# Two blocks of a transformer on one core: a GELU cut in two, constant products on TensorE ahead of turns and late loads, and the first Fourier product one unit later

## The chip, the core and the metric

One core of a Trainium2 chip runs the whole program in one launch. The metric is the time of one execution on the device in microseconds (us). TensorE (PE) multiplies, VectorE (DVE) and ScalarE (ACT) work elementwise, GpSimd (POOL) runs the scan and small parts, and SyncE (SP) issues nearly all DMAs.

## The reference, cut to what matters

Everything is float32, batch 1, 256 tokens, width 2048. `first_block` is a block with modulation, a state space mixer, attention and a gated feed forward part; `second_block` holds an attention layer over latents and context, and a Fourier layer:

```
h = modulate(rms(x, norm1_w), shift1, scale1);  u, q, k, v = split(h @ w_in)
y_ssm = glu(gelu(s5_scan(u) + d * u));  y_att = dilated_attention(q, k, v)
x = x + gate1 * (concat(y_ssm, y_att) @ w_out)
h2 = modulate(rms(x, norm2_w), shift2, scale2)
x = x + gate2 * ((silu(h2 @ w_gate) * (h2 @ w_up)) @ w_down)
... second block, layer 0: attention; layer 1:
a, b = split(h @ w_in_fourier);  o = (silu(b) * real(fft2(a))) @ w_out_fourier
x = layer_norm(alpha * x + gate * o) * g + bias
```

`gelu` is the tanh form. The modulation vectors (shift, scale, gate) are `silu(c) @ w_ada + b_ada`, with weights of 2048 x 12288. All shapes: 256 x 2048 activations, `w_in` 2048 x 4096, feed forward width 5632, Fourier width 4096 in 16 groups of 256.

## The kernel before, in words

**Units.** Each large weight is streamed from HBM in units of two 128-row tiles by 512 columns (512 KB). SP loads a unit into `raw` (a ring of 8, `load`, L186), ACT rounds it to `whi` (`high`, L192, a ring of 4), DVE subtracts to get `wlo` (`low`, L198), and PE multiplies three times: hi by hi, hi by lo, lo by hi (`multiply` L205, 12 products of 512 columns; `multiply_turned` L218, 24 products of 256 columns). `high` waits until the unit four before it has been multiplied. The order in which ACT, DVE, PE and SP take units and all other steps is written out by hand, one list per engine, and every engine works its list strictly in that order.

**Start.** The modulation weights come in 512 KB slots, and `rounds_pe` (L277) multiplies two slots per round into bank 6 (`L297`). After round 31, ACT copies the row out (`set_row_act`), PE turns it into columns (`set_turn_pe`, bank 7), and DVE adds the bias. Then `turn_pe` (L477) transposes the normed x, two tiles a round; DVE scales the result into `h32` (L500), ACT rounds it to `hh` (L507) and POOL subtracts to get `hl` (L512). Round n of the turn must be through POOL before unit n is multiplied. The same turn opens the feed forward part and the Fourier part (in `hidden_pe`, L1955: four rounds ahead of unit 0, then one behind each of the first units).

**In projection** (`in_pe`, `in_act`, `in_dve`, L1231 to L1501). 64 units of `w_in`, with the steps of the eight attention heads and of the state space mixer between them: scores (`a1_scores_pe`), maximum (`a1_max_dve`), `a1_exp_act`, `a1_prob_dve`, and so on. The GELU of half b of the mixer is `y_act` (L895): eight activations of 32 x 256 in two calls, each call four pieces for two values of j (L901). `y_act(act, 0, 2)` stands behind `high` of unit 48, ahead of `high` of unit 49. On DVE, `low` of unit 63 stands behind `a1_max_dve` of head 4. Behind unit 63, PE waits for the last evacuation (`s_inev` 8) and runs rounds 32 to 35 of the next modulation set, whose accumulator is bank 6. The slots of rounds 36 and up are loaded again as rounds 32 and up release them; in SP's list they stand behind the load of the last `w_glu` unit, which waits for `low` of unit 63.

**Feed forward and Fourier** (`Hidden`, `hidden_*`, L1590 to L2001). Chunk c: units 0 to 7 gate columns into banks 0 and 1, 8 to 15 the others into banks 2 and 3, 16 to 23 the down projection of the chunk before. In the Fourier part DVE copies banks 2 and 3 to `ub` (`hidden_up_dve`, L1740), PE multiplies 16 products with the cosine table (`hidden_dft1_pe`, L1899, `L1907`), ACT stores them (`hidden_store_act`, L1682), PE multiplies 32 more (`hidden_dft2_pe`, L1912), and DVE forms the product with the gate (`hidden_product_dve`, L1756). For chunk 0 the copy to `ub` is the last DVE step of chunk 0, the first product stands behind unit 0 of chunk 1, the store behind `high` of unit 2, the second product behind unit 3.

Of the kernel before, what the change touches and what calls it, by code (L numbers as in the profile page):

```python
# [48 lines left out]
U_IN = 0  # L49
# [49 lines left out]
def program(nc, dram, out):  # L99
# [34 lines left out]
    ones = sb(ctx, "ones", [P, P])  # L134
    cols = sb(ctx, "cols", [P, NCOLS])
# [408 lines left out]
    xn = xacc  # L544
# [349 lines left out]

    def y_act(act, b, j0):  # L895

        act.wait_ge(s_yv, b + 1)
        for j in (j0, j0 + 1):
            for pp in range(4):
                o = yT[32 * pp:32 * pp + 32, 4 * b:4 * b + 4].rearrange("p (t f) (m j) -> p t f m j", t=2, j=4)[:, :, :, :, j]  # L900
                ins = nc.scalar.activation(o, u4(b)[32 * j:32 * j + 32, :, pp::4], ACT.Gelu_apprx_tanh)  # L901
        ins.then_inc(s_yg, 1)

    def y_high(act, q):
        if q == 0:
            act.wait_ge(s_mm, U_GLU)
        act.wait_ge(s_yg, 2 * (q // 2) + 2)
        nc.scalar.copy(hh[:, 2 * q:2 * q + 2], yT[:, 2 * q:2 * q + 2]).then_inc(s_yh, 1)
# [298 lines left out]
    def in_sp(sp):  # L1207
# [21 lines left out]
        slots_sp(sp, 96, 104)  # L1229

    def in_pe(pe):  # L1231
        turn_pe(pe, 0, xn, 0, 0, 2)
        for n in range(43):
            if n < 8:
                pe.wait_ge(s_hl, n + 1)
            in_mult(pe, n)
            if n < 6:
                turn_pe(pe, 0, xn, 0, n + 2, n + 3)
            for b in range(2):
                if n == 12 + 8 * b:  # L1240
                    u_turn_pe(pe, b)
                if n == 16 + 8 * b:
                    ends_pe(pe, b)
            if n == 38:
                y_pe(pe, 0)
            if n == 40:
                a1_turn_pe(pe, 0)
# [29 lines left out]
        pe.wait_ge(s_inev, 8)  # L1277
        rounds_pe(pe, 32, 36)
        a1_pturn_pe(pe, 4)
# [31 lines left out]
    def in_act(act):  # L1311
# [31 lines left out]
        for h in range(2):  # L1343
# [3 lines left out]
            a1_qkT_act(act, h + 1)  # L1347
            high(act, U_IN + u + 3)
            if h == 1:
                in_evac(act, 5)  # L1350
# [4 lines left out]
            if h == 0:  # L1355
                y_act(act, 0, 2)
            if h:
# [61 lines left out]
    def in_dve(dve, ch):  # L1419
# [34 lines left out]
        a1_y_dve(dve, 2)  # L1454
        low(dve, U_IN + 62)
        a1_max_dve(dve, ch, 4)
        low(dve, U_IN + 63)
        a1_prob_dve(dve, ch, 4)
# [238 lines left out]
    def hidden_act(act, H, c):  # L1697
        first = isinstance(c, int) and c == 0
# [3 lines left out]
        for j in range(4 if first else 0, 16 if first else 24):  # L1702
# [22 lines left out]
            if not first or j > 4:  # L1725
                high(act, **H.unit(c, j))
            if H.fourier and c == 1 and j == 2:
                hidden_store_act(act, H, 0)
# [58 lines left out]
    def hidden_dve(dve, H, c, q=None, perq=0, lo=0):  # L1787
# [7 lines left out]
        for j in range(4 if first else 0, n):  # L1795
            if not first:
                for r in range(2):
                    if j == PARTS_AT[H.fourier][r]:
                        hidden_low_dve(dve, H, c, r)
                if second and j == 3 and not H.fourier:  # L1800
                    hidden_up_dve(dve, H, 0)
# [40 lines left out]
            if not H.fourier and not first and c <= 8 and j in (18, 20):  # L1842
                dual_sum(dve, 2 * (c - 1) + (j - 18) // 2)
        if H.fourier and first:
            hidden_up_dve(dve, H, 0)
        if q is not None and H.fourier:
# [103 lines left out]
    def hidden_pe(pe, H, c, q=None, perq=0, lo=0):  # L1950
# [3 lines left out]
        if first:  # L1954
            turn_pe(pe, k, xn, kn, 0, 4)  # L1955
        for j in range(16 if first else 24):
# [14 lines left out]
            if not first:  # L1971
                if H.fourier and c == 1 and j == 0:
                    hidden_dft1_pe(pe, H, 0)
                if H.fourier and j == 3:
                    hidden_dft2_pe(pe, H, c - 1)
                if H.fourier and j == 19:
                    hidden_dft1_pe(pe, H, c)
                if H.fourier and c == FCH - 1 and j == 21:
                    hidden_dft2_pe(pe, H, c)
# [1121 lines left out]
    def _(pe):  # L3101
# [12 lines left out]
        for k in range(4):  # L3114
            window_turn_pe(pe, 8 + 2 * k, 10 + 2 * k)
            rounds_pe(pe, 25 + k, 26 + k)
        rounds_pe(pe, 29, 32)
        set_turn_pe(pe, 0)
# [81 lines left out]
```

## Time and profile before

| | before |
|---|---|
| median of 3 runs | 2507.25 us (2505.16 to 2508.38) |
| the profiled execution | 2505.13 us, span 2503.3 us |
| PE busy | 2397.9 us, 96% of the span |
| DVE busy | 1650.0 us, 66% |
| ACT busy | 1044.6 us, 42% |
| mean granted clock of PE | 0.984 |
| DMA | 589.44 MB, 235 GB/s mean |

The span runs from the first to the last instruction. The granted clock is the share of 2.4 GHz that PE was given: 1.00 or 0.50. Matmuls are pipelined, so the duration of one (0.39 us for 512 columns) is longer than the distance to the next one (0.23 us); a row that merges several gives the length of the whole run.

### The profile page before, as it was taken

How to read it: one execution, taken by the hardware profiler on the slowest of the kernel's cores; microseconds unless marked ns; L12 is line 12 of the kernel's file. 1: busy time of each engine (PE TensorE's matmuls, PEld its weight loads, DVE VectorE, ACT ScalarE, POOL GpSimd, SP SyncE). 2: the span in 40 equal slices, each digit the busy share in tenths (PEclk: the TensorE clock that was granted, in tenths of full speed). 3: DMA queues.
4: the chain of work that ended last, by engine and by line, in shares of the span. 5: the costliest groups of instructions: out<-in, count | busy, mean ns of one | idle time of the engine just before them, and what ended most of it. 6: DMA issues, size and time to landing. Idle time of an engine off the chain costs nothing.

```text
span 2503.3 us, 37893 instructions
## 1 busy us (share of the span) xinstructions
PE 2397.9 (96%) x15430; PEld 2053.1 (82%) x15430; DVE 1650.0 (66%) x1869; ACT 1044.6 (42%) x1386; POOL 220.5 (9%) x200
## 2 busy tenths in 40 slices
PE   5899989989999999999999999999979999999996
PEld 1588766569888999888998888888768999999995
DVE  8655545456888888886678566555665585765557
ACT  2444764224333343333343454444443443334432
POOL 0139700011000000000010100000012000000000
PEclk9999999999999999999999999999999999999998
DMA  9855469968999999998554754334546585766561
GB/s 388 331 159 154 146 252 374 401 229 285 356 355 355 380 350 352 348 351 298 167 185 137 236 159 129 104 104 135 169 134 200 196 283 165 240 229 185 152 189 56
DMA packets 257582, 589.44 MB, mean 235 GB/s; under 512 B 20608, under 2 KB 29824, under 8 KB 256128
## 3 DMA queue, kind: packets, MB, share of 16 engines
q1 hardware_dynamic: 257408, 587.02, 67.8%
q8 instruction: 122, 2.00, 0.3%
q14 instruction: 52, 0.43, 0.0%
HBM read 584.85 MB, written 2.10 MB: 234 GB/s over the span
## 4 chain that ended last, share of the span: by engine, by line
PE 90%; DVE 4%; DMA 3%; ACT 1%; issue 1%; POOL 1%; SPq 0%; DVEq 0%; ACTq 0%
PE psum L213 13%; PE psum L225 13%; PE psum L226 12%; PE psum L227 12%; PE psum L215 12%; PE psum L214 12%; PE psum L297 3%; DMA start_slots<-in_w_ada 2%; PE psum L2555 1%; PE psum L1907 1%; DVE wlo L202 1%; PE psum L755 1%; PE psum L487 1%; PE psum L535 1%; PE psum L1921 1%
## 5 line engine op out<-in xcount | busy, mean ns | idle before, releaser
L202 DVE TENSOR_TENSOR wlo<-raw,whi 128x1024 fp32r<-128x1024 f32 (+2 forms) x728 | 879.6, 1223 | 546.7 <-ACT whi L196 543.3
L196 ACT CAST whi<-raw 128x1024 fp32r<-128x1024 f32 (+2 forms) x728 | 738.1, 1022 | 925.4 <-PE psum L227 484.3
L225 PE MATMUL psum<-hh,whi 128*128 128x256 f32 x2688 | 759.6, 283 | 3.1 <-DVE wlo L202 2.5
L226 PE MATMUL psum<-hh,wlo 128*128 128x256 f32 x2688 | 750.5, 279 | 0.0
L227 PE MATMUL psum<-hl,whi 128*128 128x256 f32 x2688 | 750.3, 279 | 0.0
L225 PEld LDWEIGHTS psum<-hh,whi 128*128 128x128 f32 x2688 | 506.8, 189 | 19.9 <-DVE wlo L202 11.7
L227 PEld LDWEIGHTS psum<-hl,whi 128*128 128x128 f32 x2688 | 510.8, 190 | 0.0
L226 PEld LDWEIGHTS psum<-hh,wlo 128*128 128x128 f32 x2688 | 507.0, 189 | 1.9 <-issue 1.0
L213 PE MATMUL psum<-whi,hh 128*128 128x512 f32 (+1 forms) x720 | 292.6, 406 | 11.3 <-DVE wlo L202 7.7
L215 PE MATMUL psum<-whi,hl 128*128 128x512 f32 (+1 forms) x720 | 282.1, 392 | 0.0
L214 PE MATMUL psum<-wlo,hh 128*128 128x512 f32 (+1 forms) x720 | 280.7, 390 | 0.0
L213 PE MATMUL psum<-whi,hidh 128*128 128x512 f32 x544 | 216.5, 398 | 0.0
L215 PE MATMUL psum<-whi,hidl 128*128 128x512 f32 x544 | 212.0, 390 | 0.0
L214 PE MATMUL psum<-wlo,hidh 128*128 128x512 f32 x544 | 211.9, 390 | 0.0
L378 DVE SCALAR_TENSOR_TENSOR powers<-araw,cond,powers 128x1024 f32<-128x1024 f32 x150 | 192.3, 1282 | 8.4
L213 PEld LDWEIGHTS psum<-whi,hh 128*128 128x128 f32 x720 | 136.5, 190 | 62.5 <-issue 22.6
L215 PEld LDWEIGHTS psum<-whi,hl 128*128 128x128 f32 x720 | 136.5, 190 | 29.5
L214 PEld LDWEIGHTS psum<-wlo,hh 128*128 128x128 f32 x720 | 136.9, 190 | 28.5 <-issue 1.9
L475 POOL TENSOR_TENSOR rstd<-ms,mhalf 128x2 f32<-128x2 f32 x5 | 6.4, 1288 | 1553.7 <-DVE ms L2087 633.7
L213 PEld LDWEIGHTS psum<-whi,hidh 128*128 128x128 f32 x544 | 102.1, 188 | 30.8 <-issue 11.0
L215 PEld LDWEIGHTS psum<-whi,hidl 128*128 128x128 f32 x544 | 102.1, 188 | 21.8
L214 PEld LDWEIGHTS psum<-wlo,hidh 128*128 128x128 f32 x544 | 102.2, 188 | 20.7 <-issue 1.0
(394 smaller groups left out, 2400.2 us busy)
## 6 DMA issues: line engine op xcount, KB each, us to landing
araw<-in_ada_w SPq DMA_DIRECT2D x128, 512.0 KB, 6.4
raw<-in_w_in_fourier SPq DMA_DIRECT2D x128, 512.0 KB, 4.1
raw<-in_w_ffn_gate SPq DMA_DIRECT2D x88, 512.0 KB, 8.8
raw<-in_w_ffn_up SPq DMA_DIRECT2D x88, 512.0 KB, 7.5
raw<-in_w_ffn_down SPq DMA_DIRECT2D x88, 512.0 KB, 9.8
raw<-in_w_in_attn SPq DMA_DIRECT2D x88, 512.0 KB, 4.3
araw<-in_w_ada SPq DMA_DIRECT2D x80, 512.0 KB, 7.1
start_slots<-in_w_ada SPq DMA_DIRECT2D x64, 512.0 KB, 8.2
```

Source lines behind the costliest of these rows:

```text
L196: nc.scalar.copy(whi[:, u % SPLITS, 0:kn, 0:w], raw[:, u % RING, 0:kn, 0:w]).then_inc(s_hi, 1)
L202: nc.vector.tensor_tensor(wlo[:, u % SPLITS, 0:kn, 0:w], raw[:, u % RING, 0:kn, 0:w], whi[:, u % SPLITS, 0:kn, 0:w].bitcast(F32), ALU.subt ...
L213: nc.tensor.matmul(o, ah[:, kt + k, a], h, start=(kt + k == first_kt), stop=False)
L214: nc.tensor.matmul(o, ah[:, kt + k, a], lw, start=False, stop=False)
L215: ins = nc.tensor.matmul(o, al[:, kt + k, a], h, start=False, stop=(kt + k == last_kt))
L225: nc.tensor.matmul(o, h, hh[:, kt + k], start=(kt + k == 0 and f % 2 == 0), stop=False)
L226: nc.tensor.matmul(o, lw, hh[:, kt + k], start=False, stop=False)
L227: ins = nc.tensor.matmul(o, h, hl[:, kt + k], start=False, stop=(kt + k == KT - 1 and f % 2 == 1))
L297: ins = nc.tensor.matmul(psum[32 * g:32 * g + 32, SET_BANKS[st][0]], condz[:, vectors - 1, kt, 3 - pi:35 - pi], slot(2 * r + e)[0][:, half ...
L378: ins = nc.vector.scalar_tensor_tensor(out=acc, in0=w, scalar=s, in1=acc, op0=ALU.mult, op1=ALU.add)
L487: ins = nc.tensor.transpose(psum[:, banks[r % 2], j * S + t * P:j * S + t * P + P], xn[:, t, kt * P:(kt + 1) * P], ident[:])
L535: nc.tensor.matmul(psum[:, bank], ones[:], diag[:, r % 2], start=True, stop=True).then_inc(s_grow, 1)
```

## The change

`warm_pe(pe, n, bank)` multiplies `ones` (128 x 128) by the first 256 of the column constants n times into a bank that nothing reads at that time. It is called on PE at these places: two products ahead of each of the rounds 29, 30 and 31 and three behind; five behind the first two rounds of the first turn; two, four and three around rounds 32 to 35; 16 ahead of the feed forward turn and 33 ahead of the Fourier turn, and two and five between their rounds 1 and 2. The GELU call for j = 2, 3 of half 0 becomes two calls of four activations. DVE takes `low` of unit 63 ahead of the maximum of head 4. In the Fourier part the copy to `ub` of chunk 0 moves into chunk 1 ahead of `low` of unit 2, the first product behind unit 1, the store behind `high` of unit 4, the second product behind unit 4.

```diff
-    def y_act(act, b, j0):
+    def y_act(act, b, j0, n=2):
...
-        for j in (j0, j0 + 1):
+        for j in range(j0, j0 + n):
...
-        act.wait_ge(s_yg, 2 * (q // 2) + 2)
+        act.wait_ge(s_yg, 2 * (q // 2) + 3)
...
+    def warm_pe(pe, n, bank):
+
+        for _ in range(n):
+            nc.tensor.matmul(psum[:, bank, 0:256], ones[:], cols[:, 0:256], start=True, stop=True)
+
     def in_pe(pe):
         turn_pe(pe, 0, xn, 0, 0, 2)
+        warm_pe(pe, 5, 6)
...
         pe.wait_ge(s_inev, 8)
-        rounds_pe(pe, 32, 36)
+        rounds_pe(pe, 32, 33)
+        warm_pe(pe, 2, 7)
+        rounds_pe(pe, 33, 34)
+        warm_pe(pe, 4, 7)
+        rounds_pe(pe, 34, 36)
+        warm_pe(pe, 3, 7)
         a1_pturn_pe(pe, 4)
...
             high(act, U_IN + u + 3)
+            if h == 0:
+                y_act(act, 0, 2, 1)
             if h == 1:
                 in_evac(act, 5)
             a1_pT_act(act, h)
...
             if h == 0:
-                y_act(act, 0, 2)
+                y_act(act, 0, 3, 1)
...
         low(dve, U_IN + 62)
+        low(dve, U_IN + 63)
         a1_max_dve(dve, ch, 4)
-        low(dve, U_IN + 63)
...
-            if H.fourier and c == 1 and j == 2:
+            if H.fourier and c == 1 and j == 4:
                 hidden_store_act(act, H, 0)
...
-                if second and j == 3 and not H.fourier:
+                if second and j == (2 if H.fourier else 3):
                     hidden_up_dve(dve, H, 0)
...
-        if H.fourier and first:
-            hidden_up_dve(dve, H, 0)
...
         if first:
-            turn_pe(pe, k, xn, kn, 0, 4)
+            warm_pe(pe, 33 if H.fourier else 16, 6)
+            turn_pe(pe, k, xn, kn, 0, 2)
+            warm_pe(pe, 5 if H.fourier else 2, 6)
+            turn_pe(pe, k, xn, kn, 2, 4)
...
-                if H.fourier and c == 1 and j == 0:
+                if H.fourier and c == 1 and j == 1:
                     hidden_dft1_pe(pe, H, 0)
-                if H.fourier and j == 3:
+                if H.fourier and j == (4 if c == 1 else 3):
                     hidden_dft2_pe(pe, H, c - 1)
...
-        rounds_pe(pe, 29, 32)
+        pe.wait_ge(s_ones, 1)
+        for r in range(29, 32):
+            warm_pe(pe, 2, 7)
+            rounds_pe(pe, r, r + 1)
+        warm_pe(pe, 3, 7)
         set_turn_pe(pe, 0)
```

## Rows read from the trace of the kernel before

**Rows 1.** The page: engine, busy us (share of the span), instructions.
```profile
PE 2397.9 (96%) x15430; PEld 2053.1 (82%) x15430; DVE 1650.0 (66%) x1869; ACT 1044.6 (42%) x1386; POOL 220.5 (9%) x200
```

**Rows 2.** Waits of PE, 0 to 345: us in total, times, longest.
```profile
PE psum L213 <- DVE wlo L202: 7.7, 4, 2.9
```

**Rows 3.** Waits of PE from 1862 to the end.
```profile
PE psum L225 <- DVE wlo L202: 2.5, 1, 2.5
```

**Rows 4.** Timeline of ACT, 240 to 304: start us, us, instruction, [idle before <- releaser].
```profile
269.57 0.59 ACT L1029 COPY xacc<-psum 128x512 f32<-128x512 f32 x1 [3.19 <-PE psum L1021]
...
273.24 1.28 ACT L901 ACT_TABLE_LOAD   x1
274.53 5.34 ACT L901 ACTIVATE bt_x<-proj 32x256 f32<-32x256 f32 x8
279.90 1.04 ACT L196 CAST whi<-raw 128x1024 fp32r<-128x1024 f32 x1
...
282.25 0.91 ACT L1001 ACTIVATE xacc<-xacc,neg 128x256 f32<-128x256 f32 x2
```

**Rows 5.** Timeline of PE, same stretch: units 49 and 50.
```profile
282.37 0.50 PE L213 MATMUL psum<-whi,hh 128*128 128x512 f32 x1 [2.61 <-DVE wlo L202]
...
287.17 0.50 PE L213 MATMUL psum<-whi,hh 128*128 128x512 f32 x1 [1.77 <-DVE wlo L202]
```

**Rows 6.** Timeline of all engines around unit 63, 332 to 366.
```profile
341.73 0.75 DVE L991 SCALAR_TENSOR_TENSOR xacc<-x,cols,psum 128x512 f32<-128x512 f32 x1 [5.53 <-PE psum L981]
...
343.31 1.22 DVE L202 TENSOR_TENSOR wlo<-raw,whi 128x1024 fp32r<-128x1024 f32 x1
...
344.59 0.50 PE L213 MATMUL psum<-whi,hh 128*128 128x512 f32 x1 [2.90 <-DVE wlo L202]
...
346.50 0.63 PE L214 MATMUL psum<-wlo,hh 128*128 128x512 f32 x1
...
348.87 1.01 ACT L1189 COPY proj<-psum 128x1024 f32<-128x1024 f32 x1 [4.53 <-PE psum L215]
...
350.24 1.93 PE L297 MATMUL psum<-araw,cond_windows 128*32 128x512 f32 x16
...
357.25 1.07 PE L297 MATMUL psum<-araw,cond_windows 128*32 128x512 f32 x8 [1.92 <-DMA araw<-in_w_ada]
```

**Rows 7.** Windows: stretch, busy us and count of each engine, PEclk, DMA share, GB/s.
```profile
104.00:105.00 1.00, 0.00 (x0) 0.00 (x0) 1.00 (x2) 0.58 (x1) 0.34 (x1) 0.50 1.06 391
...
289.00:290.00 1.00, 1.00 (x3) 0.76 (x3) 1.00 (x2) 0.00 (x0) 1.00 (x1) 0.50 0.85 328
...
350.00:351.00 1.00, 1.00 (x11) 0.36 (x13) 0.52 (x2) 0.61 (x2) 0.00 (x0) 1.00 0.00 0
...
480.00:500.00 20.00, 20.00 (x103) 11.85 (x102) 9.76 (x9) 5.24 (x5) 0.00 (x0) 1.00 1.04 402
...
1886.00:1887.00 1.00, 1.00 (x7) 1.00 (x6) 1.00 (x2) 0.07 (x1) 0.85 (x1) 0.50 0.00 0
```

**Rows 8.** Timeline of PE, 2440 to 2445: sixteen products of 256 float32 columns.
```profile
2441.42 3.61 PE L1907 MATMUL psum<-dft,ub 128*128 128x256 f32 x16
2444.68 0.58 PE L213 MATMUL psum<-whi,hidh 128*128 128x512 f32 x1
```

**Rows 9.** Timeline of PE at the three turns, 102, 550 and 1878.
```profile
102.11 1.07 PE L487 MATMUL psum<-ident,xacc 128*128 128x128 f32 x8
106.16 0.80 PE L213 MATMUL psum<-whi,hh 128*128 128x512 f32 x1 [2.98 <-POOL hl L512]
...
550.30 1.97 PE L487 MATMUL psum<-ident,xacc 128*128 128x128 f32 x8 [7.59 <-DVE xacc L467]
...
1878.21 1.97 PE L487 MATMUL psum<-ident,xacc 128*128 128x128 f32 x8 [15.16 <-DVE xacc L2876]
```

**Rows 10.** Timeline of DVE and PE at the start of Fourier chunk 1.
```profile
1932.14 1.22 DVE L1748 COPY ub<-psum 128x1024 f32<-128x1024 f32 x1 [8.52 <-PE psum L227]
...
1934.65 0.35 PE L225 MATMUL psum<-hh,whi 128*128 128x256 f32 x1 [2.54 <-DVE wlo L202]
```

## The prediction

> **What bounds the kernel now.** I read the page first: PE is busy 96% of the span, no other engine over 66% [rows 1]. So what shortens the run is PE's idle time, and the time in which its products run at half speed. Then I read the waits of PE by stretch. In the feed forward part there are none. Up to 345 PE waited 7.7 us for `low` in four waits [rows 2], and behind the start of the Fourier part 2.54 us in one [rows 3, 10]. Beside these it waits at the three turns: 2.98, 7.59 and 15.16 us [rows 9]. Last I read windows of one us for the granted clock. It is 1.00 (2.4 GHz) nearly everywhere and 0.50 (1.2 GHz) in a few stretches, each behind such a wait [rows 7]. At 0.50 two `L214` or `L213` products of 512 columns lie 0.43 us apart and at 1.00 they lie 0.23 us apart, so a product loses 0.20 us.
>
> **GELU in two pieces.** Before, ACT idles 3.19 us ahead of the copy of head 0 at 269.57, then takes the table load (1.28) and all eight activations (5.34) in one go, and `high` of unit 49 comes only at 279.90 [rows 4]. PE has finished unit 48 and its small steps by 279.76 (282.37 - 2.61) and stands 2.61 us; unit 50 then stands another 1.77 us, because the exponentials of head 1 came at 282.25, and DVE forms the probabilities of that head ahead of `low` of unit 50 [rows 4, 5]. After the change the load and four activations (1.28 + 2.67 = 3.95 us) go into the 3.19 us of idle time. The copy, `high` 47 and `high` 48 come 0.8 us later, and unit 47 some 0.3 us later. The second piece needs no load, if only copies and casts stand between: in rows 4 the load stands only where the function changes, not behind the copy at 269.57 or the casts. ACT is then through `high` 49 at about 277.8, 3.1 us earlier than 280.9. Unit 49 starts as soon as PE is free, at 279.9 rather than 282.4. The exponentials come at 279.1 instead of 282.25, 3.1 us earlier, and what hangs on them, `low` of unit 50 too, moves with them: unit 50 starts at 284.1 rather than 287.17. Still 1.5 us of waiting stay ahead of it, now on DVE's order alone. Gain 3.1 us. From below: 2.3, if only the wait of unit 49 less the delay of unit 47 is won; from above 4.4, both waits. I take 3.1, since it follows from ACT's own order.
>
> The Trainium skill ("ScalarE: Activation LUTs", What ACT_TABLE_LOAD costs) puts a drain of about 1.38 us on top of each load. Here the next activation starts 1.29 us after the load's start (273.24 to 274.53) [rows 4], so the trace disagrees. With the drain the first piece would end 1.4 us later and the gain would be about 1.7 us.
>
> **Unit 63.** Its `low` stands behind the maximum of head 4, which waits for scores that PE makes behind unit 62: DVE stood 5.53 us, started the maximum at 341.73, and took `low` at 343.31 [rows 6]. PE waited 2.90 us and began at 344.59. From 346.07 the clock was 0.50, so six of the twelve products (one of them is the row at 346.50, 0.63 long) lost 0.20 us each, 1.2 us, and the small products behind them another 0.4. In the new order `low` 63 runs in DVE's 5.53 us, PE goes on from 341.35 without a wait and ends unit 63 at about 344.1, not 348.65: 4.5 us. What is next is ACT's evacuation, `L1189` at 348.87 [rows 6]. It stands behind the exponentials of head 4, which end at 344.34 (348.87 less its idle time of 4.53) and do not move (the maximum starts at 341.73 as before). So it starts at 344.4, 4.5 us earlier, rounds 32 to 35 start at 345.4 instead of 350.24, and round 36 hangs on a DMA that SP issues when round 32 is done: 357.25 becomes 352.4. SP is there in time, since the load ahead of it waited for `low` 63. The nine constant products lie between round 32 and that DMA: PE has 3.6 us of rounds and 1.1 us of head steps in a stretch of 7.0 us. They cost 1.8 us (next part) and fit. They cost that much if the DMA were there at once. From 366 to 530 the DMAs run at a share of 1.04 and 402 GB/s [rows 7], so there a gain survives only if the transfers start earlier too. They do: before, the queues stood empty at 350 (0.00) [rows 7], waiting for round 32, and this moves with PE. Gain 4.5 us; bounds 0 (the full DMA stretch eats all) and 4.9.
>
> **Fourier.** The copy to `ub` waited 8.52 us for unit 15 and held `low` of the next unit behind it. PE stood 2.54 us at 1934.65 [rows 10]. Now `low` of units 0 and 1 run in those 8.52 us, PE goes on at once and the copy lies beside unit 0. The first product now starts behind unit 1, 5.6 us after unit 15, and the copy needs 1.22. The store stands behind `high` 4 and is over 5 us ahead of the second product (units 2, 3 and 4 take 8.5 us, the first product's end plus four copies 2.1 us). DVE's product with the gate, ahead of `low` 7, starts one unit later: 3.4 us for it and 1.2 for `low` against 5.6 us of units 5 and 6. So 1 us of cover is left, and if it were gone the cost would be what is missing. SP's queue isn't touched. Gain 2.5 us, bounds 1.5 and 2.54.
>
> **The constant products.** There are 79: 9 in the start, 5 in its turn, 9 in rounds 32 to 35, 18 and 38 at the other turns. Sixteen float32 products of 256 columns take 2444.68 - 2441.42 = 3.26 us up to the next product, 0.204 us each [rows 8], at half clock 0.41. So 33 take 6.7 us of the 15.16 us wait, 16 take 3.3 of 7.59, and 5 take 1.0 (or 2.0) of 2.98 [rows 9]. All are over well before what PE waits for; the three behind round 31 take 0.6 us beside ACT's copy of the row (0.59). Their cost is 0, bounds 0 and 0.5 us.
>
> What they may give is clock. At 0.50 the kernel lost: unit 0 of the start (106.16 on [rows 9]) ten products, 2.0 us; unit 50 [rows 5, 7] eight, 1.6 us; 360 to 366 about 2.0; feed forward unit 0, 12 products of 256 columns at 0.21 instead of 0.12, 1.2 us; Fourier unit 0 (the window at 1886 in [rows 7]) 2.1 us. Together 8.9 us beyond what stands above. For unit 50 the reason goes partly with the 2.61 us wait. But the big groups end long ahead of the turn: 33 products leave 8.4 us of waiting, 16 leave 4.2. Waits shorter than these (2.61 and 1.77, [rows 5]) were enough for 0.50 at 289 [rows 7]. So at the two later turns I expect little. At the start 1.0 us of products stands right behind the transposes, at 103.2; there the clock had fallen by 104 [rows 7], with PE busy on transposes to 103.18 [rows 9]. I take a third of 8.9, 3.0 us; bounds -1 (the fall comes at another moment and takes more) and 8.9.
>
> The Trainium skill ("TensorE: Matmul & The Clock Gate", Part 4, PE-mode transpose) says that transposes don't count as activity for the full clock. The start agrees: eight transposes ran to 103.18 and the clock was 0.50 at 104 [rows 7, 9]. By that rule the transposes between the constant products and unit 0 bring nothing, and the second and third turn stay as they are; its time is that of the second rival below.
>
> **Sum.** 3.1 + 4.5 + 2.5 + 3.0 - 0 = 13.1 us. The profiled execution took 2505.13 us (span 2503.3 and 1.8 around it), so 2492.0 for one like it. The median is 2.1 us above it, so I give 2507.25 - 13.1 = 2494.
>
> **The rivals.**
> - The clock is held everywhere: 3.1 + 4.5 + 2.5 + 8.9 = 19.0, 2488 us. For it: constant products stand at each of these places. Against: the 8.4 us of wait left at the Fourier turn. Chance 0.13.
> - The clock isn't held anywhere new: 10.1 us, 2497. For it: the length of the waits left and the transposes. Chance 0.25.
> - The gain at unit 63 is lost to the DMAs: between 366 and 530 they are at a share of 1.04 [rows 7], and if the slots come no earlier, PE waits there for them. 13.1 - 4.5 = 8.6, 2499. Against: the empty queue at 350. Chance 0.12.
> - A GELU table is loaded again for the second piece, and the wait at unit 50 grows back, with the clock unhelped and the DMAs full: the gain is only that of the Fourier part and a little, 2.5 to 5 us, about 2503. Chance 0.06.
> - The other side: the constant product is dearer than rows 8 say. The nearest dearer price is 0.82 us, twice for the half clock and twice if the operand of ones takes two passes more. Then 33 and 16 take 40.2 us against waits of 22.75, 17.4 us on the path, and with the 13.1 won the run is 4.3 us slower: 2511.6. It decides from 0.73 us a product ((22.75 + 13.1) / 49). Against: the row itself. Chance 0.04.
>
> **How the numbers follow.** The forecast (2494, and what lies between 2491 and 2496.5) has 0.40. The range from 2488 to 2500 takes in the clock rivals and the lost gain at unit 63. Outside are the last two, with some of the tails, under 0.2. What a measurement of this kernel can tell is about 0.2%, 5 us: faster means below 2502.2. Faster 0.90 (forecast 0.40, the first three rivals 0.50 less a little for their tails, part of the fourth), within 0.2% 0.06, slower 0.04.
>
> **What would show it.** In the profile after: no wait of PE for `low` at unit 49 and about 1.5 us at unit 50; eight GELU activations in two groups with one load ahead of the first; no wait ahead of unit 63, and the evacuation `L1189` some 7.5 us earlier than 348.87 (3.1 of them from the GELU); rounds 36 and 37 still waiting for DMAs; no wait of PE at the start of Fourier chunk 1; constant products 0.20 us apart, all inside the waits. If they are 0.4 us apart at full clock, the price is wrong, and the big groups fill the waits and hold the clock: then the first rival comes. If PE waits more for DMAs between 366 and 530 than before, the third rival holds.

## The result, and the profile after

| | before | after |
|---|---|---|
| median | 2506.2 us (4 runs, 2503.50 to 2508.38) | 2488.65 us (4 runs, 2485.01 to 2491.40) |
| ratio, 95% interval | | 0.9927 [0.9915, 0.9938] |
| profiled execution | 2505.13 us, span 2503.3 | 2490.37 us, span 2488.6 |
| mean granted clock of PE | 0.984 | 0.990 |

The ratio is 18.3 us won (0.0073 x 2506.2), between 15.5 and 21.3. The forecast was 13.1 us won, and that lies outside. The sign was right and all four gains are there. The term of the constant products was too small, because their price was wrong, and the reasoning about what they do was wrong as well.

A note on lines: `warm_pe` multiplies in L1234; L1907 of before is now L1918, L1748 is L1761, L2876 is L2890. "After" is the changed kernel, "a row" one PE instruction in the profile.

The page of after, answering to [rows 1]: PE is busy 22 us longer in a span that is 14.7 us shorter, with 158 more instructions, most of which stand in its waits.

```profile
PE 2419.9 (97%) x15588; PEld 2073.0 (83%) x15588; DVE 1652.7 (66%) x1869; ACT 1045.3 (42%) x1386; POOL 221.9 (9%) x200
```

PE's waits up to 345 us, answering to [rows 2]: of the four waits for `low`, 7.7 us, three small ones are left.

```profile
PE psum L213 <- DVE wlo L202: 1.2, 3, 0.6
```

**The GELU.** ACT, answering to [rows 4]. The load and four activations now stand ahead of the copy of head 0 (269.39), the second four stand ahead of the cast of unit 49 with no load of their own. The activation at 266.68 starts 1.30 us after the load's start.

```profile
265.38 1.28 ACT L901 ACT_TABLE_LOAD   x1
266.68 2.69 ACT L901 ACTIVATE bt_x<-proj 32x256 f32<-32x256 f32 x4
269.39 0.59 ACT L1029 COPY xacc<-psum 128x512 f32<-128x512 f32 x1
...
273.19 2.68 ACT L901 ACTIVATE bt_x<-proj 32x256 f32<-32x256 f32 x4
275.90 1.06 ACT L196 CAST whi<-raw 128x1024 fp32r<-128x1024 f32 x1
276.97 1.28 ACT L1001 ACT_TABLE_LOAD   x1
278.27 0.91 ACT L1001 ACTIVATE xacc<-xacc,neg 128x256 f32<-128x256 f32 x2
```

On PE unit 49 doesn't wait, and unit 50 waits 0.57 us, where [rows 5] had 2.61 and 1.77.

```profile
282.60 0.50 PE L213 MATMUL psum<-whi,hh 128*128 128x512 f32 x1 [0.57 <-DVE wlo L202]
```

**Unit 63.** All engines, answering to [rows 6]. The maximum of head 4 still waits for its scores, but `low` of unit 63 is done by then, PE goes on, and the evacuation starts at 338.36 instead of 348.87. Rounds 36 and 37 (349.05) find their DMA landed.

```profile
335.21 0.59 PE L213 MATMUL psum<-whi,hh 128*128 128x512 f32 x1
335.60 0.75 DVE L991 SCALAR_TENSOR_TENSOR xacc<-x,cols,psum 128x512 f32<-128x512 f32 x1 [4.39 <-PE psum L981]
...
338.36 1.01 ACT L1189 COPY proj<-psum 128x1024 f32<-128x1024 f32 x1
...
342.48 1.99 PE L1234 MATMUL psum<-cols,ones 128*128 128x256 f32 x8
...
349.05 1.92 PE L297 MATMUL psum<-araw,cond_windows 128*32 128x512 f32 x16
```

**The constants.** PE at the Fourier turn, answering to [rows 9]. The 33 products of the code are 66 rows and 14.40 us long, and fill the whole wait: 0.91 us of 15.16 is left. The five between rounds 1 and 2 are 10 rows.

```profile
1854.12 14.40 PE L1234 MATMUL psum<-cols,ones 128*128 128x256 f32 x66
1869.43 1.09 PE L487 MATMUL psum<-ident,xacc 128*128 128x128 f32 x8 [0.91 <-DVE xacc L2890]
1870.36 2.32 PE L1234 MATMUL psum<-cols,ones 128*128 128x256 f32 x10
1873.69 0.63 PE L487 MATMUL psum<-ident,xacc 128*128 128x128 f32 x4 [1.00 <-DVE h L500]
```

Windows, answering to [rows 7]: the clock column (ahead of the DMA share) is 1.00 at the start, behind unit 50 and in Fourier unit 0. In the last line it is not: this stretch of after fell to 0.50, which the same place of before did not.

```profile
104.00:105.00 1.00, 1.00 (x7) 0.90 (x6) 1.00 (x3) 0.05 (x1) 0.00 (x0) 1.00 1.04 383
289.00:290.00 1.00, 1.00 (x6) 0.84 (x5) 1.00 (x1) 1.00 (x4) 0.92 (x2) 1.00 0.93 252
...
1876.00:1877.00 1.00, 1.00 (x11) 1.00 (x11) 1.00 (x3) 0.33 (x1) 0.79 (x1) 1.00 0.01 4
...
395.00:410.00 15.00, 13.58 (x66) 9.89 (x62) 5.87 (x10) 3.49 (x5) 0.00 (x0) 0.66 1.00 386
```

PE in that stretch: two waits for late DMAs, and then the 16 small products of L324 take 3.41 us (1.85 before). Before had waits of 0.96 and 1.45 us at the same two rounds and kept its clock.

```profile
394.81 1.07 PE L297 MATMUL psum<-kt,cond_windows 128*32 128x512 f32 x8 [1.25 <-DMA kt<-in_w_ada]
397.30 1.93 PE L297 MATMUL psum<-kt,cond_windows 128*32 128x512 f32 x8 [1.42 <-DMA kt<-in_w_ada]
...
400.60 3.41 PE L324 MATMUL psum<-select,h 128*128 128x2 f32 x16
```

**Fourier chunk 1.** DVE, then PE, answering to [rows 10]: the copy lies beside unit 0, and the first product follows unit 1 with no wait on either side.

```profile
1921.26 1.23 DVE L1761 COPY ub<-psum 128x1024 f32<-128x1024 f32 x1 [3.08 <-PE psum L227]
...
1926.50 3.61 PE L1918 MATMUL psum<-dft,ub 128*128 128x256 f32 x16
```

**Where the time came from**, by the start of the same PE instruction in both profiled executions:

| up to | before | after | difference | won in this stretch |
|---|---|---|---|---|
| L820, behind the start | 160.41 | 159.40 | -1.0 | 1.0: unit 0 at full clock (2.0), less 1.0 that the turn of the row is later |
| L1037 of head 2 | 333.59 | 327.46 | -6.1 | 5.1: GELU, 3.6 of waits and 1.5 clock |
| end of unit 63 | 348.63 | 338.16 | -10.5 | 4.3: `low` of unit 63 |
| L1021 behind the unit that follows rounds 36 and 37 | 371.15 | 358.86 | -12.3 | 1.8: clock behind round 32; the waits for DMAs at 357 and 361 (4.3) are gone, and the nine products (3.9) and two small waits (0.9) stand there instead |
| feed forward turn | 550.30 | 542.75 | -7.6 | -4.7: the fall at 397 |
| end of feed forward unit 0 | 559.17 | 550.45 | -8.7 | 1.2: clock |
| end of Fourier unit 0 | 1889.32 | 1878.42 | -10.9 | 2.1: clock |
| first product, next chunk | 1997.57 | 1982.84 | -14.7 | 3.8: Fourier order |

The constants' own stretches are 1.0 + 1.8 + 1.2 + 2.1 = 6.1 us.

This table sets one execution against one, and the clock falls at other moments in other executions of the same code. The experiments below left twelve more traces, and in each stretch some of them ran the old code and some the new. The same stretches in all of them, in us:

| stretch | old code | new code |
|---|---|---|
| start to L820 | 160.4 (before), 162.3, 163.1, 163.2, 164.0 | 158.6 to 159.7 (7 traces) |
| to L1037 of head 2 | 173.2 (before), 171.5 (3 traces) | 168.0 to 168.1 (10) |
| to the end of unit 63 | 15.0 (before), 15.2, 15.5; 13.9 with the GELU cut (e3) | 10.7 (10) |
| to L1021 (358.86 in after) | 22.5 (before), 21.6 to 22.3 (4) | 20.7 to 21.0 (9) |
| feed forward turn to the end of unit 0 | 8.9 (before), 8.2 to 9.1 (4) | 7.6 to 7.7 (7) |
| Fourier turn to the end of unit 0 | 11.1 (before), 9.7, 10.8, 11.0, 11.0 | 9.0 to 9.1 (6) |
| to the first product, next chunk | 108.2 (before), 107.2, 107.2, 108.8 | 104.4 to 104.5 (10) |

Traces in which an edit changed that very place are left out of its row.

The profiled execution of before was the quickest of five at the start: its turn of the row and its transposes ran at full clock (1.95 and 1.07 us on PE). In e1, e3, e4 and e5, which have no constants there, they ran at half (e3; the others are within 0.01 us of its durations):

```profile
100.73 3.58 PE L324 MATMUL psum<-select,h 128*128 128x4 f32 x16 [0.70 <-ACT h L312]
104.17 1.95 PE L487 MATMUL psum<-ident,xacc 128*128 128x128 f32 x8
```

So the constants of the start are worth 3.5 us on the mean of these traces and not 1.0. Around units 49 and 50 it was the slowest of four. By the means of the table the constants give 3.5 + 1.2 + 1.0 + 1.7 = 7.4 us, of which the fall at 397 takes back 4.5 to 5.1 in the executions that have it.

### The profile page after: what moved, and what is told of

Read it like the earlier page. It is cut to its first block, busy times and chain, and to the rows that moved or that the text cites. A ratio compares the mean times of both kernels' runs of the same rounds, so it can differ in the third digit from the quotient of the medians.

```text
span 2488.6 us, 38209 instructions
## 1 busy us (share of the span) xinstructions
PE 2419.9 (97%) x15588; PEld 2073.0 (83%) x15588; DVE 1652.7 (66%) x1869; ACT 1045.3 (42%) x1386; POOL 221.9 (9%) x200
## 4 chain that ended last, share of the span: by engine, by line
PE 90%; DVE 4%; DMA 2%; ACT 2%; issue 1%; POOL 1%; SPq 0%; DVEq 0%; ACTq 0%
PE psum L213 13%; PE psum L225 13%; PE psum L227 12%; PE psum L226 12%; PE psum L215 12%; PE psum L214 12%; PE psum L297 3%; DMA start_slots<-in_w_ada 2%; PE psum L2569 1%; PE psum L1918 1%; DVE wlo L202 1%; PE psum L755 1%; PE psum L535 1%; PE psum L1932 1%; PE psum L882 1%
```

## The experiments

Ratios are to the kernel before, with 95% intervals; one us is 0.0004. Intervals are some 0.002 to 0.0025 wide, so versions within about 4 us of each other aren't told apart by their ratios, and there I read the trace. Each trace is one execution.

### One part at a time

**e1.** All of the change, but `warm_pe` issues nothing.

```diff
     def warm_pe(pe, n, bank):
-        for _ in range(n):
-            nc.tensor.matmul(psum[:, bank, 0:256], ones[:], cols[:, 0:256], start=True, stop=True)
+        pass
```

> The changed kernel with none of the 79 constant products; the GELU pieces, unit 63 and the Fourier order stay. Theory A (each float32 product runs as two instructions, 0.43 us, so the groups fill the waits and hold the clock): the clock falls again at the start, near 350 and at the two later turns, 0.98 mean, and the time is 11 to 13 us under the kernel before, about 2495, 6 us over the changed one. Rival B (the gain comes from the waits taken away, and the clock is a matter of when it happens to fall): within 2 us of the changed kernel, 2488.

Measured: 2493.19 us, 0.9950 [0.9937, 0.9964], 12.5 us won. Against after (0.9927) the constants are worth 5.8 us, by the two intervals 1 to 10. The window over the Fourier turn shows what they did; 20 us at a mean clock of 0.55 and half of it idle:

```profile
1863.00:1883.00 20.00, 9.60 (x50) 8.72 (x51) 15.22 (x23) 5.71 (x7) 7.85 (x7) 0.55 0.34 106
```

Behind unit 50 (289) the clock was 1.00 without any constant. None of the ten traces with the cut GELU has a fall there, and all four without it have one, e2 with its constants too: there the shorter waits did it.

**e2.** The kernel before with the 79 constant products and nothing else (`warm_pe` and its calls as in the change).

> The kernel before with the 79 constant products and nothing else. Theory A: unit 0 of the start, of the feed forward part and of the Fourier part run at the full clock: 2.0 + 1.2 + 2.1 us, 2.0 more near 360, less 1.0 us of delay at the start: 5 to 7 us faster than the kernel before, about 2500. Rival B: no difference of more than 2 us.

Measured: 2497.86 us, 0.9976 [0.9966, 0.9986], 6.0 us won (3.5 to 8.5). With e1 (5.8), the term of the clock is some 6 us, twice the forecast's 3.0. The traces fit: 7.4 us, less the fall near 397 where it comes.

**e3, e4, e5.** The kernel before with one edit each: GELU cut in two; `low` of unit 63 ahead of the maximum; Fourier order.

```diff
# e3
-                y_act(act, 0, 2)
+                y_act(act, 0, 3, 1)      # and y_act(act, 0, 2, 1) ahead of the copy of head 0
# e4
         low(dve, U_IN + 62)
+        low(dve, U_IN + 63)
         a1_max_dve(dve, ch, 4)
-        low(dve, U_IN + 63)
# e5
-                if H.fourier and c == 1 and j == 0:
+                if H.fourier and c == 1 and j == 1:
                     hidden_dft1_pe(pe, H, 0)   # with the copy, the store and the second product
```

> The kernel before with the GELU of half 0 in two calls alone. Theory A: PE's wait at unit 49 is gone, the one at unit 50 is 1.5 us or less, and where the clock no longer falls at 288 another 1.6 us are won: 3 to 5 us faster, about 2502. Rival C (what ACT wins here is lost at unit 63, whose wait grows): 0 us.

> The kernel before with low of unit 63 ahead of the maximum of head 4 alone. Theory A: unit 63 follows at once, 4.5 us are won at 350, and 1 to 3 of them are lost until 540, where the transfers run at full share: 2 to 4.5 us faster at the end, about 2503. Rival D (the transfers give nothing back): the whole 4.5 us stay.

> The kernel before with the Fourier order alone (copy to ub, first product, store, second product one or two units later). The two traces so far: PE's wait of 2.54 us goes, and chunk 1 ran another 1.2 us faster in the changed kernel. Theory A: 2.5 to 4 us faster, about 2503, and the units of chunk 1 behind the second product 0.34 us per three products. Rival E: 2.5 us only, the pace of 0.353 us stays.

| | median | ratio | won | forecast |
|---|---|---|---|---|
| e3 GELU | 2500.35 | 0.9981 [0.9972, 0.9990] | 4.8 | 3.1 (+ up to 1.6 of clock) |
| e4 unit 63 | 2502.10 | 0.9986 [0.9977, 0.9995] | 3.5 | 4.5 |
| e5 Fourier | 2501.37 | 0.9978 [0.9970, 0.9987] | 5.5 | 2.5 |

Alone they won 13.8 us, together (e1) 12.5: the parts add up within the measurement. Each of the three is right in its sign and place.

For e3 the trace shows two parts. The stretch to L1037 of head 2 takes 168.1 us, against 171.5 in e2, e4 and e5, which have the old GELU: 3.5 us of waits. The 173.2 of before are 1.7 us more, from the moment of the clock's fall. In before it fell during unit 50 (288.0 to 291.4), which cost that much. In the other three it fell during unit 49, and since unit 50 had to wait for its `low` in any case, it cost nothing. PE of e4, where unit 50 then waits 0.26 us and not 1.77:

```profile
288.64 0.63 PE L213 MATMUL psum<-whi,hh 128*128 128x512 f32 x1
...
290.70 0.50 PE L213 MATMUL psum<-whi,hh 128*128 128x512 f32 x1 [0.26 <-DVE wlo L202]
```

e5 won more than the 2.54 us of the wait that it removes: its expectation (2.5 to 4) was missed by the median, though its interval (3.3 to 7.5) overlaps. The traces don't show the surplus as the order's. From the end of unit 0 to the first product of the next chunk e5 takes 104.41 us against 108.25 in before, 3.8 less. But e2 and e3, which have the order of before, take 107.2: against them the new order is worth 2.8 us. The other 1.0 us is mostly the pace of the multiplications in the one profiled execution of before. Behind its second Fourier product the triples (three products of 256 columns, one row each) came 0.353 us apart up to the next chunk. In all thirteen other traces, e2, e3 and e4 with the old order among them, they came 0.340 apart. The clock is 1.00 behind that product in all of them; the 108.8 of e4 in the table above has its cause ahead of it, a fall of 3.4 us at 1931. Why the pace of one execution differs isn't settled, and neither is what e5 won by time beyond 2.8.

### What a product costs

**e7.** 66 constant products ahead of the Fourier turn instead of 33.

```diff
-            warm_pe(pe, 33 if H.fourier else 16, 6)
+            warm_pe(pe, 66 if H.fourier else 16, 6)
```

> The changed kernel with 66 constant products ahead of the Fourier turn instead of 33. It measures the price of one on the path: by theory A (0.43 us each) 66 take 28.3 us against a wait of about 15.2, so 13 us are added, about 2502; by the price of the prediction (0.204 us) they would take 13.5 us and fit, about 2488.

Measured: 2497.62 us, 0.9968 [0.9956, 0.9981], 10.3 us slower than after (6 to 15 by the two intervals). PE at the turn:

```profile
1854.18 28.65 PE L1234 MATMUL psum<-cols,ones 128*128 128x256 f32 x132
1882.67 1.04 PE L487 MATMUL psum<-ident,xacc 128*128 128x128 f32 x8
1883.54 2.32 PE L1234 MATMUL psum<-cols,ones 128*128 128x256 f32 x10
1885.70 1.04 PE L487 MATMUL psum<-ident,xacc 128*128 128x128 f32 x8
```

28.5 us for 66 products is 0.43 each, on the path once the wait is full. The turn starts 13.2 us later than in after, but round 2 then stands ready and unit 0 ends only 10.9 us later. So the price of a product is 0.43 us at full clock, and most of the excess is paid.

**e6.** 16 and 8 instead of 33 and 16 ahead of the turns, so that the waits aren't full.

```diff
-            warm_pe(pe, 33 if H.fourier else 16, 6)
+            warm_pe(pe, 16 if H.fourier else 8, 6)
```

> The changed kernel with 16 constant products ahead of the Fourier turn instead of 33 and 8 ahead of the feed forward turn instead of 16: they end where the prediction had thought that 33 and 16 end. Theory A: 8.3 us of wait stay at the Fourier turn and 4.2 at the other, the clock is 0.50 when unit 0 comes, and 2.1 and about 1 us are lost: about 2491. Rival F (a few products close to the turn do it): as the changed kernel.

Measured: 2486.12 us, 0.9920 [0.9906, 0.9934]. My theory A, that the big group has to fill the wait, fell: nothing was lost. PE at the turn:

```profile
1851.74 5.34 PE L1234 MATMUL psum<-cols,ones 128*128 128x256 f32 x24
1865.33 1.97 PE L487 MATMUL psum<-ident,xacc 128*128 128x128 f32 x8 [8.25 <-DVE xacc L2890]
1867.09 3.38 PE L1234 MATMUL psum<-cols,ones 128*128 128x256 f32 x10
1870.30 1.04 PE L487 MATMUL psum<-ident,xacc 128*128 128x128 f32 x8
```

After the 8.25 us of waiting the transposes run at half speed (1.97 us for 8 rows), the first of the five products too (rows 0.427 us apart, then 0.216), and the transposes behind them at full speed (1.04). Unit 0 ends 9.0 us after the turn's start, as in after.

### Which group of constants does the work

**e10 and e11.** Only the small groups (5 and 2, between rounds 1 and 2), and only the big ones (33 and 16).

```diff
# e10
-            warm_pe(pe, 33 if H.fourier else 16, 6)
# e11
-            warm_pe(pe, 5 if H.fourier else 2, 6)
```

> The changed kernel without the 33 and the 16 products ahead of the two later turns; the five and the two between their rounds 1 and 2 stay. With half of the big group the clock had fallen and was back before unit 0. Theory G (the small group brings the clock back): as the changed kernel, 2487 to 2489. Theory A (the big group holds it): 2 to 3 us slower, about 2491.

> The changed kernel with the 33 and 16 products and without the five and the two between rounds 1 and 2 of the later turns. Theory G: the clock falls between the turn's rounds or early in unit 0 in part of the executions, 1 to 2 us slower, about 2490. Theory A: as the changed kernel.

Measured: e10 2485.91 us, 0.9918 [0.9906, 0.9930]; e11 2488.53 us, 0.9928 [0.9915, 0.9941]. Their intervals against before overlap. Run against run e10 lies lower (its five times are 2485.65 to 2487.47, those of e11 2487.45 to 2491.20), but the profiled execution of e11 also lost 4.0 us between 405 and 430, with a DMA wait of 2.42 us and a fall of the clock at 411. What the groups do is read from the trace. PE of e10, then of e11:

```profile
1864.83 1.97 PE L487 MATMUL psum<-ident,xacc 128*128 128x128 f32 x8 [15.15 <-DVE xacc L2889]
1866.59 3.81 PE L1234 MATMUL psum<-cols,ones 128*128 128x256 f32 x10
1870.23 1.04 PE L487 MATMUL psum<-ident,xacc 128*128 128x128 f32 x8
...
1873.86 0.60 PE L487 MATMUL psum<-ident,xacc 128*128 128x128 f32 x4
```

```profile
1868.19 1.10 PE L487 MATMUL psum<-ident,xacc 128*128 128x128 f32 x8 [0.92 <-DVE xacc L2889]
1872.45 1.99 PE L487 MATMUL psum<-ident,xacc 128*128 128x128 f32 x8 [3.16 <-DVE h L500]
...
1879.14 0.60 PE L487 MATMUL psum<-ident,xacc 128*128 128x128 f32 x4
```

With the whole wait of 15.15 us left, five products between the rounds bring the clock back before unit 0: 9.0 us from the turn's start to the end of unit 0, as in after. With the wait full but 3.16 us free between the rounds, the clock falls there and unit 0 runs at half speed: 10.95 us, as before (11.1). The five traces without constants lie between 9.7 and 11.1 there, and the six with five products between the rounds that ended in the wait at 9.0 to 9.1, with 33, 16 or no products ahead of the turn. So at the Fourier turn all of the gain is the small group's. At the feed forward turn the same stretch takes 8.9 us before, 7.7 after, 7.6 in e10 and 8.5 in e11.

**e12.** Without the nine products around rounds 29 to 31.

```diff
-        for r in range(29, 32):
-            warm_pe(pe, 2, 7)
-            rounds_pe(pe, r, r + 1)
-        warm_pe(pe, 3, 7)
+        rounds_pe(pe, 29, 32)
```

> The changed kernel without the nine products around rounds 29 to 31; the five behind the first two rounds of the start's turn stay. In the profiled pair the start's turn came 1.0 us later with the nine, and unit 0 ran 2.0 us faster. Theory A (the nine hold the clock through the turn): the clock is 0.50 in part of unit 0, 1 us slower. Rival (the five do it, as between the later turns): the 1.0 us of delay is saved, 0 to 1 us faster.

Measured: 2488.47 us, 0.9927 [0.9915, 0.9939], as after. PE at the start:

```profile
100.73 3.26 PE L324 MATMUL psum<-select,h 128*128 128x4 f32 x16 [0.74 <-issue]
103.85 1.95 PE L487 MATMUL psum<-ident,xacc 128*128 128x128 f32 x8
105.59 3.45 PE L1234 MATMUL psum<-cols,ones 128*128 128x256 f32 x10
108.69 0.58 PE L213 MATMUL psum<-whi,hh 128*128 128x512 f32 x1
```

The turn of the row starts 0.7 us earlier (100.73 against 101.39), but it and the transposes run at half speed, and the five, half of them at half speed, end so late that unit 0 starts at 108.69 instead of 107.15. L820 comes at 161.0, between the traces with both groups (158.6 to 159.7) and those with neither (160.4 to 164.0). A difference of 1.5 to 2 us is less than the intervals can tell.

**e9.** One product instead of three behind round 31, and two and three ahead of rounds 50 and 51, where the clock fell at 397.

```diff
-        warm_pe(pe, 3, 7)
+        warm_pe(pe, 1, 7)
         set_turn_pe(pe, 0)
...
-        rounds_pe(pe, 48, 52)
+        rounds_pe(pe, 48, 50)
+        warm_pe(pe, 2, 7)
+        rounds_pe(pe, 50, 51)
+        warm_pe(pe, 3, 7)
+        rounds_pe(pe, 51, 52)
```

> The changed kernel with two constant products ahead of round 50 and three ahead of round 51, where PE waited 1.25 and 1.42 us for DMAs and the clock fell at 397 for 11 us, and with one product behind round 31 in place of three. Theory A: the clock stays 1.00 between 390 and 410, which is worth up to 4.6 us in executions like the profiled one and less on the mean, since others of the changed kernel had a clock of 0.997; the turn of the start comes 0.6 us earlier: 2 to 4 us under the changed kernel, about 2485.5. Rival: the products delay the rounds and nothing is won, 2488.

Measured: 2485.98 us, 0.9924 [0.9909, 0.9940]; five runs lie at 2484.87 to 2486.33 and one at 2497.77. The window shows the place without a fall (compare 0.66 in after):

```profile
385.00:410.00 25.00, 24.41 (x158) 15.86 (x156) 13.19 (x20) 9.25 (x14) 0.00 (x0) 1.00 1.00 384
```

The time isn't apart from that of after. The fall comes in some executions and not in others: the profiled ones of after, e2, e7 and e8 had it. Those of e6, e10, e11 and e12, with the same constants at this place, had not, nor had before, e1 and e3 to e5. By the start of the same PE instructions it costs 4.5 to 5.1 us. Where it came, the profiled execution lies above the median of its kernel (e2 2500.79 against 2497.86, e7 2501.26 against 2497.62, e8 2491.50 against 2486.66); in e6, e10 and e12 it doesn't, by more than 0.2. So this trace of e9 would not show that the edit keeps the clock, and how much it wins in the median stays open. The length of the two waits doesn't sort the executions either: e8 fell behind 0.64 and 1.45 us, and e12 did not behind 1.13 and 1.44. The fall came in four of the eight traces with the constants of after around it and in none of the five without any; whether they bring it about isn't shown.

**e8.** At the two later turns, transposes of a constant in place of the products: 126 and 61 for the big groups, 19 and 8 for the small ones.

```diff
+    def warm_turns(pe, n, bank):
+        for _ in range(n):
+            nc.tensor.transpose(psum[:, bank, 0:P], ones[:], ident[:])
...
-            warm_pe(pe, 33 if H.fourier else 16, 6)
+            warm_turns(pe, 126 if H.fourier else 61, 6)
...
-            warm_pe(pe, 5 if H.fourier else 2, 6)
+            warm_turns(pe, 19 if H.fourier else 8, 6)
```

> The changed kernel with transposes of a constant (128 x 128) in place of the constant products at the two later turns, as many as take the same time at full clock: 126 and 19 at the Fourier turn, 61 and 8 at the other. If transposes hold the clock as products do, the time is that of the changed kernel, 2488. If they don't, the clock falls to 0.50 while they run, they take twice as long, 28 and 14 us against waits of 15.2 and 7.6, and the time is 18 to 22 us over the changed kernel, about 2508.

Measured: 2486.66 us, 0.9924 [0.9911, 0.9937], as after. PE, and the window inside it:

```profile
1855.24 13.92 PE L1239 MATMUL psum<-ident,ones 128*128 128x128 f32 x126
1870.56 1.09 PE L487 MATMUL psum<-ident,xacc 128*128 128x128 f32 x8 [1.40 <-DVE xacc L2895]
```

```profile
1855.00:1865.00 10.00, 10.00 (x92) 9.89 (x91) 8.99 (x8) 7.24 (x10) 3.34 (x3) 1.00 0.01 2
```

126 transposes in a row ran at 0.11 us each with the clock at 1.00 throughout, and unit 0 ended 9.0 us after the turn's start. At the feed forward turn, with eight transposes between the rounds, the clock did fall for some 3 us from 547 (from the turn to the end of unit 0 it took 9.2 us, after 7.7). So in this execution the transposes did at the Fourier turn what the products did, and at the feed forward turn they didn't.

## Why the prediction was wrong, point by point

**The step that failed: the price of a constant product, and with it the clock's term.** The view of [rows 8] groups 16 rows, 3.26 us. I divided by 16 and wrote "0.204 us each". `hidden_dft1_pe` issues eight products there (the text ahead of the prediction calls them 16), and each float32 product is two rows. The page of after shows it by count: 158 rows for 79 products, 15430 + 158 = 15588. The price is 0.43 us at full clock (e7) and 0.85 at half (the first rows of the five products of e10 lie 0.427 us apart, two a product; the last three, behind the clock's return, 0.216). With the waits of [rows 9] that price gave "33 products leave 8.4 us of waiting", and from it followed: "at the two later turns I expect little", and so a third of 8.9 us. In fact the groups fill 14.3 and 7.0 us, the clock was held or came back at every place that the forecast had named, and the term measured 6 us (e2 6.0, e1 5.8). The last part of the prediction had named this case: "if they are 0.4 us apart at full clock, the price is wrong [...] then the first rival comes". The first rival's 2488 came, within a us, but that is luck in part. The clock's term is 6 and not its 8.9; at the Fourier turn the big group didn't do it; and the other three gains were larger than the 10.1 us that it had for them.

The Trainium skill ("FP8 and Floating Point Precision", TensorE Precision Notes) says that true float32 takes four passes through the array. 4 x 256 columns at 2.4 GHz are an estimated 0.427 us by that page, and the trace agrees with 0.43.

**The reasoning behind it failed too, and e6 and e10 show that.** Even with the price right I would have said that the big groups must fill the waits, since a wait left over lets the clock fall and nothing is won. The clock does fall in the wait (0.50 in e10 up to about 1869.5), but what counts is where it stands when unit 0 begins, and five products between the rounds bring it back by then. They cost next to nothing, as round 2 waits for DVE there anyway. In e10 round 2 starts 5.40 us after the turn does (4.25 before), but runs at full speed, and unit 0 starts 6.19 us after it (1871.02 - 1864.83), before 6.16.

**The transposes' rule.** I wrote that by the Trainium skill ("TensorE: Matmul & The Clock Gate", Part 4, PE-mode transpose) the transposes between the constants and unit 0 bring nothing, and that the start agrees. e8 disagrees: 13.92 us of nothing but transposes at a clock of 1.00. What I took for agreement, 0.50 at 104 behind eight transposes, shows nothing by itself: ahead of them PE had waited 1.10 and 0.70 us, behind them 2.98. The rival built on it (2497, chance 0.25) was wrong.

**GELU: forecast 3.1, came 3.5 of waits; 5.1 against the one trace of before, 4.8 alone (e3, 2.5 to 7.0).** The order came out as worked: one load, unit 49 without a wait, exponentials at 278.27 (279.1 in the working). One size was off: unit 50 waits 0.57 us, not 1.5. So 3.8 us of waiting went, and 3.5 are left after the delay of units 47 and 48. With both waits small the clock stays at 1.00 at 289, also in e1 and e3, without constants there. I had put these 1.6 us under the constants and cut them to a third; they belong to this edit, but only in executions where the fall comes as late as in before. The load costs its 1.28 us and no more (266.68 - 265.38 = 1.30), as the forecast took it from the rows. No second load came, so that rival is out.

**Unit 63: forecast 4.5, came 4.3 in the trace and 3.5 alone (e4; 1.3 to 5.8).** The evacuation stands 10.5 us earlier than 348.87, of which 6.1 came with the stretches before it; I had said 7.5. The other 3.0 are the start (1.0) and the 5.1 of the GELU's stretch, where I had 3.1. One detail was wrong: rounds 36 and 37 don't wait for their DMA. The nine products, at their true price, are 3.9 us and filled that time. The third rival (the gain lost to DMAs between 366 and 530) didn't come: PE waited 2.4 us for DMAs there before and 2.7 after, and in e4 the 2.6 us that it is ahead at 371 are still there at the feed forward turn (2.9). But behind the DMA waits at 395 and 397 the clock fell in this execution, and that gave back 4.7 us.

**Fourier: forecast 2.5, came 3.8 against the one trace of before, 2.8 against e2 and e3, and 5.5 alone (3.3 to 7.5).** No wait, the store and the second product in time, as worked out. The 1.0 us between 2.8 and 3.8 is the slow pace of the triples in before's trace, which e2, e3 and e4 don't have; it isn't a gain of the order.

**Cost of the constants: forecast 0 to 0.5.** The three behind round 31 are 1.3 us, not 0.6, and stand ahead of the turn of the row, which starts 1.08 us later (100.31, then 101.39); a part of that is round 31's own DMA, 0.46 later. Against before's trace this is a cost. Against e1, e3, e4 and e5 it is none, as there the row and the transposes ran at half clock and unit 0 started at 108.3 to 109.4 (107.15 in after). The rest of the constants lie in waits. The rival of the other side, 0.82 us a product and slower from 0.73 on, was on the right track in its sign: with 0.43 the price was double the forecast, but 33 x 0.43 = 14.2 just fits in 15.16 and 16 x 0.43 = 6.9 in 7.59. e7 shows what a count beyond that does: 10.3 us.

**Sum.** Against the one trace of before: 5.1 + 4.3 + 3.8 + 6.1 = 19.3 us, less 4.7 for the fall at 397, is the 14.7 us of the profiled pair but for rounding. By the means of all traces: 3.9 + 4.5 + 3.5 + 7.4 = 19.3, and with the fall in half of the executions 16.9, an estimate that lies within the 15.5 to 21.3 of the ratio. That the two ways give the same 19.3 ahead of the fall is chance: before's trace shows too little for the start and too much for the other stretches.

What stays open: in which executions the clock falls behind the DMA waits of rounds 50 and 51, and why the triples of Fourier chunk 1 came at another pace in one. Of the versions run, e10 (small groups alone) has the lowest ratio, 0.9918, and needs 49 products fewer; by these intervals it isn't apart from after.

## What to carry to other kernels

Before a price is taken from a grouped row, count the instructions against what the code issues: here one float32 product is two rows, and the error of a factor two changed which rival came. One trace of the kernel before is one execution: it was up to 3.6 us off other traces of the same code in its start, 1.7 around unit 50 and 1.0 in one chunk, as much as the single gains that are to be read. To have PE at full speed behind a long wait, it isn't needed to fill the wait: a few products right ahead of the work, in a gap that PE had anyway, did it here. Filling the wait won no more, and the 33 products leave 0.9 us before they cost time.

## What the hardware showed that I had not expected

- A float32 product of 128 x 128 by 256 columns runs as two instructions, 0.216 us apart at full and 0.427 at half clock: 0.43 and 0.85 us a product (e7, e10).
- The granted clock stayed at 1.00 through 126 transposes in 13.92 us.
- Behind a wait of 15.15 us eight transposes took 1.97 us at half speed. Five products took 3.81, all but the last three of their ten rows at half speed, and the eight transposes behind them 1.04, at full speed (e10).
- Behind waits of 1.25 and 1.42 us, 2.5 us apart, the clock fell in one execution, behind 0.64 and 1.45 in another (e8); behind 1.13 and 1.44 at the same place it did not (e12).
- The same code at the same clock of 1.00 ran its triples of 256 columns 0.353 us apart in one execution (before) and 0.340 in three others (e2, e3, e4).
- Of the clock's falls at one place only some cost time: during unit 50 it cost 1.7 us (before), during unit 49, with a wait ahead of unit 50, nothing (e2, e4, e5).
